# A trunk step in hand-scheduled engine queues: unrotated queries of two attention branches projected feature-wise, stores issued by GpSimd

## The reference

```
qkv_sb, qkv_fox, f_logit, qkv_dsa, q_idx, k_idx, w_idx, gate_logit = split(h @ w_in)   # h 384 x 1024
q_*, k_*, v_* = 384 x (6 heads x 64)      # for each of sb, fox, dsa
q_dsa, k_dsa, q_idx, k_idx = rotary(..., pos)
new = (k_sb, v_sb, k_fox, v_fox, log_f, k_dsa, v_dsa, k_idx)   # all are outputs
```

## Time and profile before

| | us |
|---|---|
| median of 3 runs | 2321.64 (2321.53 to 2325.78) |
| the profiled execution's own time | 2322.41 |
| its span | 2320.4 |
| PE busy | 2295.2 (99%) |
| VectorE busy | 1230.8 (53%) |
| ScalarE busy | 545.3 (24%) |
| GpSimd busy | 71.0 (3%) |

### The profile page before, as it was taken

One profiled execution on the slowest core, in us unless ns is written; L12 is line 12 of the kernel. 1 busy time (PEld: TensorE's weight loads), 2 busy tenths in 40 slices (PEclk: granted clock), 3 DMA queues, 4 the chain that ended last, 5 costly groups with the idle time before them and its releaser, 6 DMA issues.

```text
span 2320.4 us, 41137 instructions
## 1 busy us (share of the span) xinstructions
PE 2295.2 (99%) x16907; PEld 2047.5 (88%) x16907; DVE 1230.8 (53%) x2671; ACT 545.3 (24%) x1321; POOL 71.0 (3%) x116
## 2 busy tenths in 40 slices
PE   8999999999999999999999999999999999999999
PEld 6999997886688699999999999977856886999999
DVE  4666442633656446665375664426345754666743
ACT  2000022113564231001130010311235642400011
POOL 0000000000022000000000000000000220000000
PEclk9999999999999999999999999999999999999999
DMA  9454334782489353443435533547725984233332
GB/s 339 163 175 162 100 128 151 224 276 90 149 294 348 129 195 110 145 146 100 137 134 176 176 129 117 168 134 238 258 73 176 337 303 150 74 109 109 100 123 78
DMA packets 300466, 390.09 MB, mean 168 GB/s; under 512 B 31078, under 2 KB 250972, under 8 KB 300280
## 3 DMA queue, kind: packets, MB, share of 16 engines
q1 hardware_dynamic: 281688, 337.82, 43.3%
q0 software_dynamic: 11840, 42.30, 5.2%
q10 hardware_dynamic: 6752, 7.33, 0.9%
HBM read 375.30 MB, written 12.12 MB: 167 GB/s over the span
## 4 chain that ended last, share of the span: by engine, by line
PE 94%; DMA 2%; SPq 2%; ACT 1%; DVE 1%; issue 1%; ACTq 0%; DVEq 0%
PE PS L779 32%; PE PS L875 13%; PE PS L1055 6%; PE PS L1328 4%; PE PS L956 4%; PE PS L1007 4%; PE PS L719 3%; PE PS L1146 3%; PE PS L1227 3%; PE PS L923 2%; PE PS L931 2%; PE PS L1029 2%; DMA BIG<-w_ada 2%; PE PS L1381 2%; PE PS L1358 2%; PE PS L1267 2%
## 5 line engine op out<-in xcount | busy, mean ns | idle before, releaser
L779 PE MATMUL PS<-OT,RING 128*128 128x192 f32 x1280 | 234.2, 326 | 0.0
L779 PE MATMUL PS<-H,RING 128*128 128x192 f32 x1280 | 222.1, 327 | 0.0
L779 PE MATMUL PS<-OT,QR 128*128 128x192 f32 x1280 | 221.1, 326 | 0.0
L779 PEld LDWEIGHTS PS<-OT,RING 128*128 128x128 f32 x1280 | 212.4, 190 | 0.0
L779 PEld LDWEIGHTS PS<-H,RING 128*128 128x128 f32 x1280 | 208.4, 190 | 3.8 <-issue 3.2
L779 PEld LDWEIGHTS PS<-OT,QR 128*128 128x128 f32 x1280 | 210.2, 190 | 0.0
L1495 ACT ACTIVATE QR<-QR 128x384 f32<-128x384 f32 x80 | 41.8, 523 | 533.8 <-DVE QR L2094 533.8
L1055 PE MATMUL PS<-H,RING 128*128 128x384 f32 x480 | 161.1, 490 | 0.0
L1055 PEld LDWEIGHTS PS<-H,RING 128*128 128x128 f32 x480 | 88.9, 190 | 60.2 <-issue 3.7
L779 PE MATMUL PS<-H,QR 128*128 128x192 f32 x640 | 117.1, 326 | 0.0
L1950 DVE TENSOR_TENSOR OT<-OT 128x192 f32<-128x192 f32 x154 | 53.0, 355 | 103.2 <-ACT OT L1466 93.0
(11 more groups left out here) (340 smaller groups left out, 3996.5 us busy)
## 6 DMA issues: line engine op xcount, KB each, us to landing
RING<-ffn_w_in SPq DMA_DIRECT2D x80, 1024.0 KB, 7.3
RING<-w_in SPq DMA_DIRECT2D x64, 768.0 KB, 6.3
QR<-w_ada SPq DMA_DIRECT2D x34, 1024.0 KB, 9.7
BIG<-w_ada SPq DMA_DIRECT2D x34, 1024.0 KB, 10.3
RING<-ffn_w_out SPq DMA_DIRECT2D x32, 768.0 KB, 4.6
RING<-ffn_w_out SPq DMA_DIRECT2D x32, 640.0 KB, 5.4
QR<-cache_sb_v POOLq DMA_DIRECT2D x16, 768.0 KB, 5.2
QKT<-cache_sb_k SPq DMA_DIRECT2D x16, 768.0 KB, 5.8
```

The source lines that it names most:

```text
L779: mm = pe.matmul(PS[:, bank, GROUP[g]], a[:, k, :], x[:, k, :], start=(k == 0), stop=(k == 3))
```

## The change

The queries of `sb` and `fox` (groups 0 and 3) leave the list of token-major units. In their place stand `QPAIRS` = 3 units ahead of the others. Pair unit `a` takes 128 features of sb q and 128 of fox q (256 features x 1024 x all 384 tokens) by the same seven products, with weights (or their sums `SWP`, made by `pair_sums`) stationary and `H` (or its sums `THP`, made once per layer by `half_sums`) moving. The result has features on partitions and isn't turned; ScalarE copies it to `QKT` and `QBLK` after the turns. The token-major units are `TOKEN_PROJ` = 8, 1, 2, 4, 5. The 8 units are numbered u = 0 to 7, the pairs first.

The turns are 6 in place of 9: three for dsa (q and k), three that turn fox k (on the q side's bank) and sb k. The modulation units stand after units 0 and 2 to 6. The stores are issued by GpSimd in one list. On SyncE the cache loads are issued at i = 2, the write of `g_s` behind the load `gates(1)`.

```diff
-N_IN, N_OUT, N_PROJ, N_GATE, N_BRANCH, N_WOUT = 11, 8, 10, 8, 4, 2
+N_IN, N_OUT, N_PROJ, N_GATE, N_BRANCH, N_WOUT = 11, 8, 11, 8, 4, 2
-ADA_TILE, ADA_UNIT = (4, 8), range(6)
+ADA_TILE, ADA_UNIT = (4, 8), (0, 2, 3, 4, 5, 6)
-PROJ = [6, 7, 9, 8, 0, 1, 2, 3, 4, 5]
+PROJ = [6, 7, 9]
+TOKEN_PROJ = [8, 1, 2, 4, 5]
+QPAIRS, TOKENS = NPAIR, len(TOKEN_PROJ)
+SEVEN_PROJ = QPAIRS + TOKENS
+TURNS = 2 * TT
...
                         sp.wait_ge(p2_ready, l * SEVEN_PROJ + i - 4)
+                    if kind is None:
+                        d, a = ring(l, r, KD, 2 * P), i - PLAIN_PROJ
+                        load(l, r, [(d[:, :, z * P:(z + 1) * P], w[:, :, COL_QKV[z] + a * P:COL_QKV[z] + (a + 1) * P]) for z in (SB, FOX)])
...
-                    if i == 4:
+                    if i == 2:
                         for c in range(PC):
                             sp.dma_start(LFC[:, c * 48:c * 48 + 48].rearrange("p (b h) -> p b h", b=NB),
...
-                    if i == 9:
-                        sp.wait_ge(g_ready, l * 2 + 2)
-                        sp.dma_start(g_p, RSTD[0:NH, 0:NPROMPT]).then_inc(g_stored, 16)
...
+                gates(1)
+                sp.wait_ge(g_ready, l * 2 + 2)
+                sp.dma_start(g_p, RSTD[0:NH, 0:NPROMPT]).then_inc(g_stored, 16)
...
+                    if u < QPAIRS:
+                        w, sw = ring(l, R_PROJ + PLAIN_PROJ + u, KD, 2 * P), SWP[u % 2]
+                        product(0, 0, w[:, lo, 0:P], H[:, lo, GROUP[0]])
+                        product(0, 1, w[:, hi, 0:P], H[:, hi, GROUP[0]]).then_inc(pp_ready, 1)
...
+                        pe.wait_ge(sh_ready, 2 * l + 1)
+                        pe.wait_ge(tp_ready, 2 * g + 2)
+                        if g:
+                            pe.wait_ge(pp_taken, 4 * g)
+                        product(3, 0, sw[:, 1], THP[:, 1]).then_inc(pp_ready, 1)
+                        product(1, 0, sw[:, 0], THP[:, 0])
+                        product(1, 1, w[:, lo, P:2 * P], THP[:, 2]).then_inc(pp_ready, 2)
+                        product(2, 0, sw[:, 2], H[:, hi, GROUP[1]])
+                        product(2, 1, w[:, hi, P:2 * P], THP[:, 3]).then_inc(p2_ready, 1)
...
-                for r in range(NBR):
-                    for tt in range(TT):
...
+                for i in range(TURNS):
+                    tt = i % TT
+                    if i == 1:
+                        pe.wait_ge(pp_taken, 4 * SEVEN_PROJ * (l + 1) - 2)
+                        pe.wait_ge(p2_taken, TOKENS * (l + 1))
+                    if i > 1:
+                        pe.wait_ge(q_taken, l * Q_TAKEN + i - 1)
...
+                for r in (SB, FOX):
+                    src = qr(r * TT * 2 * MIX, TT * 2 * MIX).rearrange("p (a c) -> p a c", a=NPAIR)
+                    link(A(QKT[:, r, 0, :, :], src[:, :, 0:NPROMPT], ACT.Copy))
+                    ins = sample_queries(r, src[:, :, NPROMPT:T])
...
-                    act.dma_start(t[f"o_{name}_p"][l].rearrange("o (t p) h d -> p (o t) (h d)", p=P),
-                                  src[:, r, 0:2, cols]).then_inc(stored, 16)
...
+                    pool.dma_start(t[f"o_{name}_p"][l].rearrange("o (t p) h d -> p (o t) (h d)", p=P),
+                                   src[:, r, 0:2, cols]).then_inc(stored, 16)
...
+                def half_sums():
+                    b11, b12, b21, b22 = (H[:, 4 * i:4 * i + 4, GROUP[g]] for i in range(2) for g in range(2))
...
+                def pair_sums(u):
+                    n = l * RINGS + R_PROJ + PLAIN_PROJ + u
+                    dve.wait_ge(slot_full[n % 2], 32 * (n // 2 + 1))
+                    if u > 1:
+                        dve.wait_ge(p2_ready, l * SEVEN_PROJ + u - 1)
...
+                    V.tensor_tensor(sw[:, 0], a21, a22, ALU.add).then_inc(vch, 1)
+                    V.tensor_tensor(a21, a11, a21, ALU.subtract).then_inc(vch, 1)
...
+                    V.tensor_tensor(sw[:, 1], sw[:, 0], a11, ALU.subtract).then_inc(vch, 1)
...
+                    V.tensor_tensor(sw[:, 2], a12, sw[:, 1], ALU.subtract).then_inc(tp_ready, 2)
...
                 for u in range(SEVEN_PROJ):
+                    if u + 1 < QPAIRS:
+                        pair_sums(u + 1)
...
+                    assembled(u)
+                    if u + 1 == QPAIRS:
+                        projected_sums(u + 1)
```

More of the change, by code:

```diff
@@ L255, in program @@
         P1P, U2P, U43P = qr(QX + 1248, HALF), qr(QX + 1248 + HALF, HALF), qr(QX + 1248 + T, T)
[L256 removed]
+        TP = [x.rearrange("p (v k c) -> p v k c", v=4, k=KD // 2) for x in (QKTR[:, 0:3072], big(1152, 3072))]
+        THP = QKTR[:, 0:3072].rearrange("p (v k t) -> p v k t", v=4, k=KD // 2)
+        SWP = [big(1152 + 1536 * i, 1536).rearrange("p (v k c) -> p v k c", v=3, k=KD // 2) for i in range(2)]
         SH = [RING[:, 4096 * (v // 2) + 3072 + 512 * (v % 2):4096 * (v // 2) + 3584 + 512 * (v % 2)] for v in range(3)]
@@ L599, in gates @@
                     load(l, r, by_k(l, r, w, COL_GATE + g * MIX, MIX))
-                for g in range(1, 4):
-                    gates(g)
+                gates(1)
+                sp.wait_ge(g_ready, l * 2 + 2)
+                sp.dma_start(g_p, RSTD[0:NH, 0:NPROMPT]).then_inc(g_stored, 16)
+                sp.dma_start(g_s.rearrange("(g t) k -> g t k", t=NT),
+                             GX[0:48, :][:, None, :].to_broadcast([48, NT, KEYS])).then_inc(gs_stored, 16)
+                gates(2)
+                gates(3)
                 sp.wait_ge(g_stored, l * 16 + 16)
@@ L1021, in _ @@
[L1021 to L1029, removed]
@@ L1062, in _ @@
                 pe.wait_ge(gt_copied, l + 1)
-                n = l * NBR * TT
-                for r in range(NBR):
-                    for tt in range(TT):
[L1066 to L1079, removed]
+                for i in range(TURNS):
[5 more added lines that the diff above has]
+                        pe.wait_ge(q_taken, l * Q_TAKEN + i - 1)
+                    for a in range(NPAIR):
+                        src = QK[:, DSA, tt, a * P:(a + 1) * P] if i < TT else QK[:, FOX, tt, MIX + a * P:MIX + (a + 1) * P]
+                        mm = pe.transpose(PS[:, turn_bank(i), a * P:(a + 1) * P], src, IDENT[:, :])
+                    mm.then_inc(q_turned, 1)
+                    if i > 1:
+                        pe.wait_ge(k_taken, l * TURNS + i - 1)
+                    for a in range(NPAIR):
+                        mm = pe.transpose(PS[:, turn_bank(i) + 1, a * P:(a + 1) * P],
+                                          QK[:, DSA if i < TT else SB, tt, MIX + a * P:MIX + (a + 1) * P], IDENT[:, :])
+                    mm.then_inc(k_turned, 1)
                 pe.wait_ge(pp_taken, 4 * SEVEN_PROJ * (l + 1))
@@ L1644, in _ @@
[L1644 to L1657, removed]
+                begin()
@@ new lines, in sample_queries @@
+                def sample_queries(r, src):
+                    src = src.rearrange("p a (b t) -> p a b t", b=NB)
+                    link(A(QBLK[0:64, r, :, :, 0:NT], src[0:64], ACT.Copy, scale=SCALE))
+                    return A(QBLK[64:128, r, :, :, NT:2 * NT], src[64:128], ACT.Copy, scale=SCALE)
+                for i in range(TURNS):
+                    tt = i % TT
+                    act.wait_ge(q_turned, l * TURNS + i + 1)
+                    src = PS[:, turn_bank(i), 0:MIX].rearrange("p (a t) -> p a t", a=NPAIR)
+                    if tt < 2:
+                        ins = A(QKT[:, DSA if i < TT else FOX, i // TT, :, tt * P:(tt + 1) * P], src, ACT.Copy)
+                    elif i < TT:
+                        ins = sample_queries(DSA, src)
+                    else:
+                        ins = A(KNT[FOX].rearrange("p (b a) t -> p a b t", b=NB),
+                                src.rearrange("p a (b t) -> p a b t", b=NB), ACT.Copy)
+                    ins.then_inc(q_taken, 1)
```

205 lines of the change are left out of this document (128 added, 77 removed).

## The result

| | before | after |
|---|---|---|
| median, us | 2323.23 (4 runs) | 2335.86 (4 runs, 2334.4 to 2337.24) |
| ratio | | 1.0058 (95%: 1.0045 to 1.007) |
| profiled execution, its span | 2322.41, 2320.4 | 2335.73, 2333.8 |

The change makes the kernel 0.58% slower, 12.6 us by the medians, where I had forecast 0.43% faster. The profiled execution took 13.3 us more than that of before.

What follows compares the result with a forecast made beforehand. PE, busy 99% of the span, was taken as the bound. Units -2.6, turns -7.1, modulation stop +2.6 and stops that go -2.9 gave -10.0 us: median 2321.6 to 2311.6 us, range 2309.5 to 2315.5 (8 in 10: 2308.5 to 2317.0).

Steps and rivals of the forecast that it cites:

- The step that failed: SyncE's queue: third pair's weights issued about 423.3, sums by 432, wanted at 434.8, so free; later token units unchanged.
- Rival 2: Cache loads hold SyncE 14.4 us, first pair's weights 5.4 us late: 8.2 us more, 2319.8 us; chance 0.12.
- rival 3: First pair's weights land 15.0 us after issue, 9.8 us late in each layer: adds 17 us, 2328.6 us; chance 0.04.
- the 9.5 us: VectorE's wait for weights in a unit before the change, cited for putting its pair work (four sums, five reads) at nothing.
- Units: PE's projection: three pair units (27.63 us) replace two query units (28.92 us): -1.29 us per layer, -2.6 in all.
- Turns: PE's transposes after the projection, 36 in place of 54: 7.92 to 4.35 us, -3.57 per layer, -7.1 in all.
- Modulation stop behind pair 0: PE waits for modulation weights behind the first pair's products: 0.6 us in layer 0, 2.0 in layer 1, +2.6 in all.
- the lower end: Modulation stops of 0 and 1.2 us, if the pair's 512-byte pieces move at 361 GB/s.
- Stops that go: PE's three present waits for modulation weights, 1.0 us in layer 0 and 1.9 in layer 1, vanish: -2.9 us.
- First pair: Its weights land at 411 to 413.5, PE wants them at 413.83; about 1 us of margin, cost nothing.
- ScalarE's six copies: Extra copies after the last unit, 3.7 us, done at 8.4 when PE asks at 9.5: free by 1.1 us.
- Stores: GpSimd's stores and the memset behind them, wanted by PE at about 15.4 after the last unit: free by over 4 us.

Runs made afterwards that it cites:

- experiment 1: The change with SyncE's modulation loads issued at i = 4, 5, 7, 8, 9, 10, each behind the group with the same wait: 2312.26 us, ratio to before 0.9955.
- Experiment 7: The kernel of experiment 1 with the eight cache loads back at i = 4, behind the second pair's weights and modulation: 2325.48 us, ratio to before 1.0011.
- experiment 9: The change with only GpSimd's stores of dsa k and the indexer keys moved behind those of fox k: 2327.22 us, ratio to before 1.0021.
- experiment 2: The change with the modulation units back behind units 0 to 5, SyncE's list as in the change: 2320.34 us, ratio to before 0.9988.
- experiment 4: The change with the eight forget-value loads ahead of the modulation load at i = 7 in SyncE's list: 2327.83 us, ratio to before 1.0023.
- experiment 3: The change with all stores of the new rows issued by ScalarE instead of GpSimd, in the same units: 2332.97 us, ratio to before 1.0044.

## Why the prediction was wrong

**The step that failed** is the one that put SyncE's queue at nothing behind the pairs; it cost 24.0 us at four heads, 15.4 of waiting and 8.6 of slow clock. I followed SyncE's list up to the third pair's weights ("Free"), and for the token units said only that they "are as long as before". I had put modulation unit and load apart: units "0 and 2 to 6" on PE, `proj_ada(l, i - 2)` on SyncE. What I did not do is write, beside each group in SyncE's list, the unit that the load ahead of it waits for. The rows I had quoted would have given the price: forget or cache loads hold SyncE for many us when they stand ahead of a group, and a group behind others took 10.6 us to land. Rival 2 had this mechanism at the wrong place, the first pair; rival 3 had the right sign, with 17 us for late groups in place of the 24.0 that they cost, at the first pair too and with a chance of 0.04. The same holds for VectorE: I named the 9.5 us that it waits for weights in such a unit as if they were slack, and didn't see that the read PE needs stands behind that wait.

**Units.** -1.29 us per layer: the pairs took 9.3 us with the transpose, right.

**Turns.** 4.35 us per layer forecast, 4.69 and 4.47 measured; saved 6.7 in all, not 7.1. That is 0.4 us of the sum.

**Modulation stop behind pair 0.** 0.6 and 2.0 forecast, 0.20 and 1.24 measured, near the lower end of 0 and 1.2. What 512-byte pieces cost, two stretches of the kernel after show (the last number is GB/s, the one before it the busy share of the DMA engines). In the first almost nothing but the weights of pair 2 moves, in 512-byte pieces, in the second those of unit 3, in 1536-byte pieces:

```profile
424.00:427.00 3.00, 3.00 (x36) 2.80 (x28) 0.00 (x0) 0.84 (x4) 0.00 (x0) 1.00 1.04 280
436.00:439.00 3.00, 3.00 (x21) 3.00 (x20) 2.18 (x5) 0.33 (x1) 0.87 (x2) 1.00 1.04 375
```

By the Trainium skill's rule (DMA: Bandwidth & Descriptors, Specifications) 512 bytes are enough for line rate. The trace of these stretches doesn't bear that out: with the DMA engines as busy, such pieces moved at 280 GB/s against 375. For a pair's 1.05 MB that is about 0.8 us more than at the 361 GB/s of the earlier trace rows (an estimate), as much as I had put between the lower end and my own figure.

**Stops that go.** Those three went; four larger ones, for VectorE, came. Once SyncE's list is right, one for modulation weights is back, 0.92 us at unit 6 of layer 0 (experiment 1).

**First pair.** Landed in time, 1.06 us before PE's 412.87; SyncE was free at 403.95, 10.7 us after it took up the cache loads. VectorE's first sum of that pair, after:

```profile
411.81 0.69 DVE L2383 TENSOR_TENSOR BIG<-RING 128x512 f32<-128x512 f32 x1 [32.97 <-DMA RING<-w_in]
```

The margin of about 1 us was right. Experiment 7 shows what the same cache loads cost ahead of the third pair.

**ScalarE's six copies.** 0.83, 0.52 and 0.52 us, twice. In experiment 1 they end at 535.4 and the gate tile behind which PE asks at 536.4, so my margin of 1.1 us was 1.0.

**Stores.** Free, as said, at the memset. That their place among the loads matters I had not seen (experiment 9).

**Size.** What I forecast, 2311.6 us, is what experiment 1 measured: 2312.26. Part of that is luck: the stops behind pair 0 are 0.20 and 1.46 us there, 0.9 less than forecast, and the stop of 0.92 at unit 6, which I had at nothing, makes up for it. The projection and turns of layer 0 take 118.5 us there (412.74 to 531.26), 129.0 in the change and 122.9 before.

**The clock** was missing from every rival: I priced lateness by its own length. It took another 8.6 us.

**A slip.** The low end of my own range should be 2311.6 - 1.4 = 2310.2, not 2309.5. It changes nothing here: 2335.86 lies above every rival's time.

## What to carry to other kernels

When a consumer moves in a list ordered by hand, follow each producer's list that feeds it line by line and write down what every entry waits for: an entry whose wait ends later than the next one's holds all behind it, whatever bandwidth is free. A unit left out of an alternation shifts the pairing of everything issued by index. On an engine that is the bound, price a hole of some us as the hole and, as a bound, the slow records that may follow it: here 8.6 us on 15.4 of holes.

## What the runs showed of the hardware

The granted clock after a hole of PE is no matter of its length alone. The stretch behind a hole had a mean of 0.62 after 2.77 us and 0.50 after 4.03 (after), and 0.50 after 3.90 (experiment 7); even behind the 2.60 us of experiment 2 the 64 records of a modulation unit took 3.37 us in place of 1.95. It did not fall in experiment 4 behind one of 2.67 us, and not in experiment 3 behind one of 3.35 us, where the next 16 records took 2.84 us; the stretches are of that kernel, layer 1:

```profile
1632.00:1635.30 3.30, 0.00 (x0) 0.00 (x0) 3.23 (x6) 0.28 (x1) 0.00 (x0) 1.00 0.63 186
1635.30:1639.30 4.00, 3.96 (x25) 3.97 (x26) 3.61 (x7) 1.02 (x4) 0.00 (x0) 1.00 1.05 395
```

Nor did records slow down behind the hole of 1.93 us before, or those of 1.0 to 1.5 in experiments 3 and 9. What else decides is open. Dummy matmuls in the hole kept it at 1.00 each of the four times.
